# Second mixer and norms of a two-block network: state space two steps ahead of the attention, and a norm chain with fewer steps

## The reference

```python
h = h + 0.5 * swiglu(rmsnorm_2(h, norm_ffn1[i]), ffn1_w1[i], ffn1_w3[i], ffn1_w2[i])
z = rmsnorm_2(h, norm_mix[i]) @ w_in[i]
...
o_nsa = nsa_attention(q, kc, vc, ksl, vsl, kw, vw, gates, ...)   # 8 heads of 64, 2 key groups
o_s5 = s5_mixer(u, s5_a_re[i], ..., s5_w_glu[i], s5_b_glu[i])    # 32 groups of 16 inputs, 64 complex states
h = h + jnp.concatenate([o_nsa, o_s5], axis=-1) @ w_out[i]
h = h + 0.5 * swiglu(rmsnorm_2(h, norm_ffn2[i]), ...)
gate = jax.nn.sigmoid(rmsnorm_2(h, norm_ple[i]) @ w_ple_gate[i])
h = h + gate * (p[i] @ w_ple[i])
```

## Time and profile before

| | |
|---|---|
| three runs | 3390.56, 3392.2, 3394.92 us (median 3392.2) |
| profiled execution | 3393.95 us, span 3392.1 us, mean granted clock 0.923 |
| TensorE busy | 2988.4 us (88%) |
| VectorE, ScalarE, GpSimd busy | 1167.1 (34%), 742.8 (22%), 488.1 (14%) |
| transfers | 624.63 MB, mean 184 GB/s |

### The profile page before, as it was taken

The page is one execution under the profiler, slowest core; times in us unless marked ns, Lnnn a source line. Parts: engine busy times, 40 slices in busy tenths (PEclk is TensorE's granted clock), DMA queues, the critical chain, the costliest instruction groups (busy, mean ns, idle before and its releaser), DMA issues.

```text
span 3392.1 us, 36327 instructions
## 1 busy us (share of the span) xinstructions
PE 2988.4 (88%) x15306; PEld 2045.1 (60%) x15306; DVE 1167.1 (34%) x2301; ACT 742.8 (22%) x1338; POOL 488.1 (14%) x481
## 2 busy tenths in 40 slices
PE   5989799889778899889999949999996788899987
PEld 3777655544456565474544537888555565588875
DVE  4973200000155332310000034323364883433334
ACT  4143110101032143201111123222111333322222
POOL 0000132222110043023232210000003321000000
PEclk8989799999978999889999979999997788899998
DMA  6513799999731231369999942233112002133320
GB/s 244 192 41 129 280 381 412 405 396 399 293 122 52 92 120 50 154 255 403 413 416 393 420 164 75 88 95 115 52 68 78 1 1 100 50 100 100 100 88 31
DMA packets 132025, 624.63 MB, mean 184 GB/s; under 512 B 14079, under 2 KB 85887, under 8 KB 97424
## 3 DMA queue, kind: packets, MB, share of 16 engines
q0 software_dynamic: 40160, 403.75, 29.4%
q1 hardware_dynamic: 90544, 213.49, 18.0%
q10 hardware_dynamic: 1152, 4.98, 0.4%
HBM read 615.87 MB, written 29.36 MB: 190 GB/s over the span
## 4 chain that ended last, share of the span: by engine, by line
PE 43%; DMA 7%; DVE 5%; ACT 2%; issue 1%; POOL 0%; ACTq 0%; SPq 0%; POOLq 0%; DVEq 0%
PE ps L92 42%; DMA ring<-in_exp_up,wix 6%; DVE scr L106 2%; PE ps L95 1%; ACT hT L98 1%; DVE scr L126 1%; DVE hT L114 0%; DVE xT L114 0%; DVE scr L114 0%; DVE hT_r L106 0%; DMA scr<-yrows 0%; DVE ring_r L106 0%; DMA ring<-in_cmp_w 0%; ACT scr L98 0%; POOL ring L135 0%
## 5 line engine op out<-in xcount | busy, mean ns | idle before, releaser
L92 PE MATMUL ps<-ring,scr 128*64 128x512 f32 (+3 forms) x3136 | 749.1, 569 | 64.0 <-DMA ring<-in_exp_up,wix 62.8
L92 PE MATMUL ps<-ring_r 128*128 128x512 f32 (+1 forms) x2544 | 758.9, 380 | 38.0 <-DVE hT_r L106 29.3
L92 PEld LDWEIGHTS ps<-ring_r 128*128 128x128 f32 x2544 | 474.3, 193 | 153.5 <-issue 39.1
L92 PEld LDWEIGHTS ps<-ring,scr 128*64 128x64 f32 (+2 forms) x3136 | 306.0, 160 | 421.7 <-issue 411.7
L92 PE MATMUL ps<-scr,ring 128*128 128x128 f32 (+4 forms) x3744 | 429.8, 301 | 43.1 <-DMA ring<-yrows 20.6
L92 PE MATMUL ps<-hT_r,ring_r 128*128 128x512 f32 (+1 forms) x1224 | 464.3, 379 | 0.0
L92 PEld LDWEIGHTS ps<-scr,ring 128*128 128x128 f32 (+2 forms) x3744 | 391.5, 191 | 78.8 <-issue 56.3
L106 DVE TENSOR_TENSOR scr<-scr,ps 64x512 f32<-64x512 f32 (+1 forms) x72 | 49.7, 690 | 777.0 <-ACT scr L98 462.2
L92 PEld LDWEIGHTS ps<-hT_r,ring_r 128*128 128x128 f32 x1224 | 236.9, 194 | 40.3 <-issue 2.0
L92 PE MATMUL ps<-scr_r,ring_r 128*128 128x512 f32 x1104 | 259.6, 396 | 0.6 <-DVE scr_r L106 0.6
L102 ACT ACTIVATE scr<-ps 128x512 f32<-128x512 f32 (+3 forms) x227 | 118.8, 535 | 570.7 <-PE ps L92 380.5
(11 more groups left out here) (139 smaller groups left out, 2489.9 us busy)
## 6 DMA issues: line engine op xcount, KB each, us to landing
ring<-in_ffn_w SPq DMA_DIRECT2D x66, 1024.0 KB, 5.5
ring<-in_mod_w SPq DMA_DIRECT2D x12, 2048.0 KB, 7.5
ring<-in_mod_w SPq DMA_DIRECT2D x16, 1024.0 KB, 5.0
scr<-in_mod_w SPq DMA_DIRECT2D x8, 1024.0 KB, 8.5
ring<-in_exp_gate SPq DMA_DIRECT2D x4, 2048.0 KB, 14.8
ring<-in_exp_up SPq DMA_DIRECT2D x4, 2048.0 KB, 17.2
ring<-in_exp_down SPq DMA_DIRECT2D x4, 2048.0 KB, 21.2
ring<-in_w_in SPq DMA_DIRECT2D x4, 2048.0 KB, 7.8
```

The lines of the kernel that those rows point to most:

```text
L92: return self.real.matmul(o, l, r, start=start, stop=stop) if self.real else Quiet()
```

## The change

Norms: (1) for all but x0's norm, `st.dst` is None: VectorE's scaling reads the root from PSUM, and its last `stt` lets the bank go. (2) ScalarE's Sqrt reads the sums from PSUM with scale and eps, VectorE only takes the reciprocal, and TensorE multiplies the broadcast column of it by the identity. (3) VectorE no longer adds the last squares: TensorE takes their column sums as well, on top of those of `acc`. (4) A Sqrt of one column stands at the first square. (5) TensorE passes `stage_end` without waiting for other engines, but for two stages of the attention; the router's loads wait for the norm's sums. (6) ck's scaling works in chunks of 512 and 256. Weight splits: ffn2's first two move into the output loop of the mixer; ple's job 1 is loaded first, its upper part moves ahead of ffn2's squares; its lower part stays ahead of the reciprocal, and job 0's goes behind it.

Second mixer: the v part moves behind unit 3. The state space weights come without zeros, 1.5 MB in one load, ahead of the compression weights, which both go through slot 4. TensorE does `s5_inputs(0)`, compression 0, `s5_inputs(1)`, `s5_output(0)`, compression 1, `s5_inputs(2)`, `s5_output(1)` ahead of its loop, and VectorE `s5(0)` and `s5(1)`. In the loop the state space is two steps ahead, and its output product stands right behind the scores. Two transposes run ahead in `values` instead of one. GpSimd scales the output weights once, before the loop, in six operations of 128x512. ScalarE's gelu moves ahead of `values(14)`, and the gate products wait for it tile by tile.

```diff
     def act_square(e, st, kt, a, n):
         if kt == 0:
+            if a == 0:
+                e.activation(small[:, 8:9], k("ones")[:, 0:1], ACT.Sqrt)
     def pe_norm_sum(e, st):
         o = ps.take(st.name, "sum")
-        for c in range(nt):
-            m = e.matmul(o[:, c:c + 1], st.acc[:, 128 * c:128 * c + 128], k("ones")[:, 0:1], True, True)
+        e.matmul(o[:, 0:st.T // 128], k("diag")[:, 0:128], k("ones")[:, 0:st.T // 128], True, False)
+        def columns(x, a, n, stop):
+            for j in range(n // 128):
+                c = a // 128 + j
+                m = e.matmul(o[:, c:c + 1], x[:, 128 * j:128 * j + 128], k("ones")[:, 0:1], False, stop and j == n // 128 - 1)
+            return m
+        ...
+            m = columns(st.acc[:, a:a + n], a, n, False)
+        for kt, a, n in ends:
+            if st.last(kt, a):
+                e.wait_ge(*squared.of(st.name, kt, a))
+                m = columns(st.buffer(kt, a, n), a, n, (kt, a, n) == ends[-1])
     def pe_norm_root(e, st):
+        e.wait_ge(*inverse.of(st.name))
...
-                m = e.matmul(o[:, 128 * j:128 * j + 128], k("ones"), small[:, 16 + 128 * (c % 4):144 + 128 * (c % 4)],
-                             True, True)
+                m = e.matmul(o[:, 128 * j:128 * j + 128], small[:, c:c + 1].broadcast_to([128, 128]), k("id"), True, True)
+    def root_took(st, a, last, signal, *key):
+        return ps.emptied(st.name, "root", a) if last and st.dst is None else signal.of(*key)
     def dve_norm(e, st):
+        m = small[:, 0:st.T // 128]
+        e.wait_ge(*ps.emptied(st.name, "sum"))
+        e.recip(m, m).then_inc(*inverse.up(st.name))
+    def act_norm(e, st):
+        e.wait_ge(*ps.filled(st.name, "sum"))
...
+        e.activation(small[:, 0:nt], ps.ap(st.name, "sum")[:, 0:nt], ACT.Sqrt, bias=k("eps"), scale=1.0 / (128 * st.nk)).then_inc(
+            *ps.empty(st.name, "sum"))
...
     def sp_mixer2(e):
-                (("v",), I["w_in2v"], 8, 280), ((3,), I["w_in2"][3], 8, 512),
-                (("cmp", 0), I["cmp_w1"][0], 16, 256), (("cmp", 1), I["cmp_w1"][1], 16, 256),
-                (("s5_b",), I["s5_b"], 2, 2048), (("s5_c",), I["s5_c"], 2, 2048)]):
-            weights_load(e, 5 if i % 2 else 4, ("mix", *name), src, nk, n)
+                ((3,), I["w_in2"][3], 8, 512), (("v",), I["w_in2v"], 8, 280), (("s5",), I["s5_w"], 1, 3072),
+                (("cmp", 0), I["cmp_w1"][0], 16, 256), (("cmp", 1), I["cmp_w1"][1], 16, 256)]):
+            weights_load(e, 5 if i % 2 and i < 6 else 4, ("mix", *name), src, nk, n)
     def pe_mixer2(e):
+        s5_inputs(0)
+        for br in range(2):
+            compressed(br)
+            for half in range(2):
+                ps.release("s5_in", br, half)
+            s5_inputs(br + 1)
+            s5_output(br)
+        ps.release("s5_y", 0)
...
         for n in range(18):
             if n < 16:
                 scores(n)
+            if 1 <= n < 15:
+                s5_output(n + 1)
             if n >= 2:
                 values(n - 2)
-            ...
+            if n < 14:
+                for half in range(2):
+                    ps.release("s5_in", n + 2, half)
+                if n < 13:
+                    s5_inputs(n + 3)
+            if n < 15:
+                ps.release("s5_y", n + 1)
     def act_mixer2(e):
         for n in range(18):
             if n < 16:
                 scores(n)
+            elif n == 16:
+                e.wait_ge(*ps.emptied("s5_y", 15))
+                for q in range(4):
+                    e.activation(Mx.y[q], Mx.y[q], ACT.Gelu_apprx_tanh).then_inc(*act_step.up("gelu", q))
...
+            if m in (2, 3) and upto >= 14:
+                part_upper(e, (ffn2.name, *ffn2.jobs[m - 2]))
     def dve_mixer2(e):
+        s5(0)
+        s5(1)
+        e.wait_ge(*ps.filled("vcm", 1))
+        for n in range(17):
             if n < 16:
                 scores(n)
+            if n >= 1:
                 normal(n - 1)
+            if n < 14:
+                s5(n + 2)
+            if n == 14:
                 s5_output(15)
...
+            if m in (4, 5) and upto >= 14:
+                part_lower(e, (ffn2.name, *ffn2.jobs[m - 4]))
     def pool_mixer2(e):
-        for n in range(17):
-            if n >= 1:
-                normal(n - 1)
-            if n < 4:
-                s5_scaled(n)
+        s5_scaled()
+        for n in range(16):
+            normal(n)
     def dve_ple(e):
-        part_lower(e, ("ple", 0))
         part_lower(e, ("ple", 1))
         dve_norm(e, ffn2.st)
+        part_lower(e, ("ple", 0))
```

More of the change, by code:

```diff
@@ L261, in before, with last @@
         return [o[:2] for o in self.order if o[0]][i] if i >= 0 else None
+    def last(self, kt, a):
+        return kt == self.nk - 1 and self.turn[kt, a] + len(self.sq) >= len(self.turn)
 def by_tile(nk, T):
@@ L462, in act_norm, with root, root_there @@
[L462 to L466, removed]
-        nt = st.T // 128
-        e.wait_ge(*ps.emptied(st.name, "sum"))
-        e.activation(small[:, 0:nt], small[:, 0:nt], ACT.Sqrt).then_inc(*rooted.up(st.name))
-    def act_norm_root(e, st):
-        for a, n in chunks(st.T):
+    def root(st, a, n):
+        return ps.ap(st.name, "root", a)[:, 0:n] if st.dst is None else st.dst[:, a:a + n]
+    def root_there(st, a):
+        return ps.filled(st.name, "root", a) if st.dst is None else ps.emptied(st.name, "root", a)
@@ L2226, in act_ffn @@
     def act_ffn(e, w):
-        for kind, u in w.jobs[0:0 if w is ffn1 else 2]:
-            part_upper(e, (w.name, kind, u))
         act_norm(e, w.before)
-        act_h_parts(e, w.name)
+        act_h_parts(e, w.name, w.before)
         def upper(f, f0):
@@ L2248, in act_ffn @@
                     upper(2 * u + 1, 2 * half[0])
+        if w is ffn2 and upto >= 15:
+            part_upper(e, ("ple", 1))
         for m in range(8):
@@ L2254, in dve_ffn @@
     def dve_ffn(e, w):
-        for kind, u in w.jobs[0:0 if w is ffn1 else 2]:
-            part_lower(e, (w.name, kind, u))
         dve_norm(e, w.before)
@@ L2387, in pe_mixer2 @@
         for wi, m, dst, late, j in projections():
-            if wi == 3 and m == 0:
-                rest()
             o = ps.take("mx", wi, m)
@@ L2400, in pe_mixer2, with compressed @@
                 turn_late(late)
-        e.wait_ge(*dve_step.of("windows", 1))
-        for br in range(2):
+        rest()
+        def compressed(br):
+            e.wait_ge(*dve_step.of("windows", br))
             e.wait_ge(*wr.there("mix", "cmp", br))
@@ L2866, in sp_ple @@
     def sp_ple(e):
-        for j in range(5):
+        for i, j in enumerate((1, 0, 2, 3, 4)):
             src = I["w_ple"] if j == 0 else I["w_ple_gate"][(j - 1) // 2][:, :, 256 * ((j - 1) % 2):256 * ((j - 1) % 2) + 256]
-            raw_load(e, 1 + j, ("ple", j), src)
+            raw_load(e, 1 + i, ("ple", j), src)
         for x in (act_stage, dve_stage, pe_stage):
@@ L2933, in dve_ple @@
         dve_norm(e, st_ple)
[L2934 removed]
+        e.wait_ge(*root_there(st_ple, 0))
         for kt in range(8):
[L2936 to L2937 removed]
+            i = e.stt(X(kt, 0, 512), X(kt, 0, 512), vec("nfin2", kt), root(st_ple, 0, 512), MUL, MUL)
+        i.then_inc(*root_taken(st_ple, 0, True, x_new, "out"))
     def sp_program(e):
```

225 lines of the change are left out of this document (99 added, 126 removed).

## The result

The changed kernel takes 3354.69 us (median of 4 runs, 3353.96 to 3358.89), before 3393.56 in the same comparison; the ratio is 0.9886, 95% interval 0.9869 to 0.9904, so 1.1% faster. The profiled execution took 3353.96 (span 3352.2, granted clock 0.932).

A forecast was written before the change was run, and what follows sets the result against it. TensorE's products were taken to set most of the time, with gains only where it stands still. Profiled 3393.95 - 36 (norms) + 2.6 (mixer) - 3.5 (behind the loop) = 3357.0, 1.75 above the median, so 3355 us; range 3332 to 3380.

The forecast's parts named there:

- The norms' own chains: All 13 norms, with moved weight splits: shorter way from sums to scaling, sum 37.6 us saved, taken as 36.
- m0: Norm of the first expert stage (MoE): Sqrt starts without TensorE waiting for ScalarE's stage end, 5.2 us saved.
- m1: Norm of the second expert stage (MoE): sums to scaling shortened like the first one's, 4.5 us saved.
- the six at 1.3 each: Norms x0, conv, cq, ck, fin and the last, without exposed table load: 1.3 us each, 7.8 together.
- The operand in PSUM: Second MoE norm: five scalings beside GpSimd may take 0.75 us each instead of 1.53; 3.0 of 3.9 taken.
- The rival with half of the norms hidden: Norms: other work or transfers behind, extra columns and reloaded table leave 20 us instead of 36, 3371; chance 0.17.
- The mixer before its loop: Second mixer: both compression weights through one slot, two 9.0 us waits, compressions at 13.92, first score 27 us later.
- The loop: Second mixer's 14 state space iterations: 12.5 us VectorE work plus 1.5 hand-off each, 196 us, bounds 182 and 220.
- the count of takes: Mixer loop: counting bank takes, the first wide score gets the bank VectorE's last operation frees; 1.5 us per iteration.
- The tail: Mixer after the 14 iterations: two light iterations, the last values and 2.5 us for gelu, 34 us.
- Behind the loop: First gate product after the mixer's loop: gelu and stage end already over, 3.5 us of the 3.90 gap saved.
- the dear hand-off: Mixer loop rival: TensorE stays at 1.2 GHz, 18.0 us per iteration, 3411; chance 0.04, lighter form 3383 at 0.09.

The follow-up runs named there:

- norms_only: The changed kernel with the second mixer put back as before, keeping the changed norms, stage ends and weight splits: 3362.6 us, ratio 0.9913.
- y_first: The changed kernel with VectorE's state space output operation, which frees the bank, placed ahead of four products and small carry operations: 3337.49 us, ratio 0.9834.

## Why the prediction was right, and where it was not

The time came out at 3354.69 against 3355 by two errors that cancel: that it agrees to 0.3 us is luck.

- **The norms' own chains: right in sum, less so one by one.** From the last tile to the first scaling they gain some 36, the eleven from f on 34.3 of it, and the scalings beside GpSimd 1.6: some 37 against 37.6. Singly: ffn1 2.4 (said 2.3), m0 5.2 (5.2), m1 4.5 (4.5), the norm behind the mixer 5.3 (6.2) and the one before ple 6.3 (5.3), at 1.8 (2.3). Of the six at 1.3 each, ck brought 3.9, since its second chunk no longer holds the first scaling, and fin and the last one 0.3 to 0.4: there the extra columns take back what the chain gives. f gained 2.3 and lost it behind, as said.
- **The operand in PSUM: right place, misread and too large.** I took 3.0 for five scalings that ran 7.65 and now run 3.38. I had read the mean of 1.53 as scalings that take twice as long beside GpSimd; in the trace four take 0.75 and one is held for 4.99, until GpSimd's operation ends. Until the last of the eight only 1.6 is gained, because the add that follows the five reads two operands from SBUF and is now the one that is held, for 3.33.
- **What came behind the expert stages: missed.** I let every gain before an expert stage through but f's. The two stages together took 9.8 longer than in the trace of before. The sum put this at nothing. Some 5 of it remain on the mean of ten profiles, the rest is the spread between profiles, and what sets the stages' length stays open: the router's queue is excluded for the first, and that they end with their transfers is not shown. The rival with half of the norms hidden had named a loss behind the norms, and its size was too large: in the trace 29 of the norms' 37 are left (39.9 less the mixer's 10.8), with some 1.5 that came in products between norms.
- **The mixer before its loop: right.** Two waits for weights, two compressions of 13.9 each (2548.85 to 2562.7, 2571.77 to 2585.7), the first score 50.6 behind the projections against 52.5 forecast, 24.9 lost against 27. Only the order inside was another: the state space's products run in the waits for the weights, which leave TensorE idle for 7.57 and 5.16 instead of 9 twice.
- **The loop: right mechanism, a term too dear.** The bank did what the count of takes had said: the first wide score waits for VectorE's last operation 13 times of 13. The iterations took 190 for 196: VectorE was busy 171 of it, 12.2 per iteration, not 12.5, and waited 1.4. The tail was 35.2 for 34.
- **Behind the loop: too small.** The gap of 3.90 went, as said, and the gate products ran 13.97 instead of 16.38 at a granted clock of 1.00 instead of 0.84, which I had not counted; from the last values to the last output 6.0 came where I said 3.5. With 0.9 in the projections the stretch of the mixer won 10.8, where my terms gave 0.9; some of it is due to the stage ends of the norms' half, as `norms_only` showed.

So the mixer brought some 10 more and the expert stages took some 10 back. Of the rivals, the dear hand-off had its place right: what the iteration cost over VectorE's own work was this wait. Its reason, TensorE at the 1.2 GHz level throughout the loop, did not come: the granted clock was 0.82 there, and `y_first` took the wait away at 0.81.

## What to carry to other kernels

Count which bank, slot or buffer each step takes in turn when an order changes: a wait moves from one step to another without a line of code that names it, and one operation put earlier on the engine that frees it was worth more (17 us) than the reordering itself (some 9). A mean over merged rows can hide one instruction that waits: look at the longest before pricing the others. Where two engines hand work back and forth, put first what lets the other go on. A gain ahead of a long stage is not in the sum until the stage behind it has been read, and a gain in one stretch not until the next has.

## What the runs showed of the hardware

A VectorE scaling of 128x512 with two SBUF operands, begun just behind GpSimd's 128x2048 subtraction (4.59 us), took 4.99 us: it ended with it. With one operand in PSUM it took 0.74 beside GpSimd, as it does elsewhere. The compression of 64 products of 128x62 took 7.25 us straight behind other products, at a granted clock of 1.00, and 13.8 to 13.9 behind a pause of TensorE of 1.9 to 8.1 us, at 0.50, in all twelve profiles. ScalarE's table load took 1.28 us behind an idle stretch of 2.04, and the Sqrt started 0.01 behind it. The first expert stage took from 645.6 to 655.6 us in ten profiles of kernels that differ hardly or not at all in its code.
